# Where the projection's quanta stand in the orders of TensorE, ScalarE and VectorE

## The reference

```python
xn = rmsnorm(x, norm_mix_pre)
p = (xn @ w_in).astype(f32)                      # 256 x 2048 by 2048 x 18912
...
y_a = ...   # RWKV-7 time mixing: 32 heads of 64, a recurrence over the frames
y_b = ...   # gated DeltaNet: 16 heads of 128, chunks of 64 frames, a triangular solve in each
x = x + rmsnorm((sigmoid(gA) * y_a + sigmoid(gB) * y_b) @ w_out, norm_mix_post)
x = x + rmsnorm(SwiGLU(rmsnorm(x)))              # inner width 5632
```

## Time and profile before

| | |
|---|---|
| median of 3 runs (lowest, highest) | 2269.91 us (2266.4, 2270.58) |
| the profiled execution: time, span | 2271.85 us, 2270.1 us |
| TensorE busy | 2101.4 us, 93% of the span |
| VectorE, ScalarE, GpSimd busy | 1414.1, 1083.0, 158.8 us |
| granted clock of TensorE, mean | 0.963 of full |
| units 1 to 15 begin at | 162.77, 240.75, 320.29, ... 1182.82, 1262.33 us |
| from one unit's start to the next, units 1 to 14 | 78.0 us (nine), 79.5 us (five) |

### The profile page before, as it was taken

The page is one execution under the profiler, slowest core; times in us unless marked ns, Lnnn a source line. Parts: engine busy times, 40 slices in busy tenths (PEclk is TensorE's granted clock), DMA queues, the critical chain, the costliest instruction groups (busy, mean ns, idle before and its releaser), DMA issues. The chain is left out here.

```text
span 2270.1 us, 48877 instructions
## 1 busy us (share of the span) xinstructions
PE 2101.4 (93%) x20323; PEld 1800.4 (79%) x20323; DVE 1414.1 (62%) x2786; ACT 1083.0 (48%) x2015; POOL 158.8 (7%) x277
## 2 busy tenths in 40 slices
PE   5999999999999999999999849679999999999995
PEld 5888888888888888888888737558888888878884
DVE  5568777877877787777778644444445445444444
ACT  4545555555565555546555423344444444434443
POOL 3001011011101110110111010000000000000000
PEclk9999999999999999999999859879999999999998
DMA  6654454444454454444454017156555555545552
GB/s 197 173 142 117 117 138 126 128 123 129 116 146 117 129 133 117 124 130 128 120 143 117 6 39 259 56 187 193 193 185 185 185 185 188 181 151 188 191 190 93
DMA packets 382119, 327.20 MB, mean 144 GB/s; under 512 B 11280, under 2 KB 322032, under 8 KB 375280
## 3 DMA queue, kind: packets, MB, share of 16 engines
q1 hardware_dynamic: 367872, 318.53, 47.5%
q10 hardware_dynamic: 14064, 6.04, 1.1%
HBM read 322.44 MB, written 2.10 MB: 143 GB/s over the span
## 5 line engine op out<-in xcount | busy, mean ns | idle before, releaser
L1525 DVE TENSOR_TENSOR wlo<-wr,whi 128x1024 fp32r<-128x1024 f32 x296 | 362.6, 1226 | 435.0 <-ACT whi L1520 435.0
L232 PE MATMUL ps<-hi,xh 128*128 128x384 f32 (+1 forms) x1568 | 565.6, 361 | 31.9 <-ACT pu L258 29.2
L1520 ACT ACTIVATE whi<-wr 128x1024 fp32r<-128x1024 f32 x296 | 313.7, 1061 | 492.2 <-PE ps L1538 484.1
L234 PE MATMUL ps<-hi,xl 128*128 128x384 f32 (+1 forms) x1568 | 532.8, 340 | 0.0
L233 PE MATMUL ps<-lo,xh 128*128 128x384 f32 (+1 forms) x1568 | 531.7, 339 | 0.0
L227 DVE TENSOR_TENSOR lo<-raw,hi 128x768 fp32r<-128x768 f32 (+1 forms) x400 | 378.2, 965 | 122.1 <-ACT hi L222 121.4
L222 ACT ACTIVATE hi<-raw 128x768 fp32r<-128x768 f32 (+1 forms) x400 | 327.8, 834 | 219.4 <-PE ps L234 212.7
L232 PEld LDWEIGHTS ps<-hi,xh 128*128 128x128 f32 x1568 | 297.0, 189 | 67.9 <-ACT pu L258 36.4
L1534 PE MATMUL ps<-whi,xh 128*128 128x512 f32 x832 | 328.5, 395 | 20.4 <-DVE wlo L1525 20.4
L1536 PE MATMUL ps<-wlo,xh 128*128 128x512 f32 x832 | 326.9, 393 | 0.0
L1538 PE MATMUL ps<-whi,xl 128*128 128x512 f32 x832 | 326.7, 393 | 0.0
(11 more groups left out here) (284 smaller groups left out, 2324.5 us busy)
## 6 DMA issues: line engine op xcount, KB each, us to landing
raw<-in_w_in SPq DMA_DIRECT2D x288, 512.0 KB, 5.7
wr<-in_ffn_w_gate SPq DMA_DIRECT2D x44, 1024.0 KB, 5.1
wr<-in_ffn_w_up SPq DMA_DIRECT2D x44, 1024.0 KB, 5.1
wr<-in_ffn_w_down SPq DMA_DIRECT2D x22, 2048.0 KB, 7.5
wr<-in_w_out SPq DMA_DIRECT2D x16, 1024.0 KB, 5.1
raw<-in_w_in SPq DMA_DIRECT2D x8, 448.0 KB, 7.0
xt<-in_x SPq DMA_DIRECT2D x2, 1024.0 KB, 6.2
g2s<-in_rwkv_g ACTq DMA_DIRECT2D x16, 128.0 KB, 5.7
```

The lines of the kernel that those rows point to most:

```text
L232: nc.tensor.matmul(o, xh[:, kc, xs], high, start=kc == 0, stop=False)
L234: return nc.tensor.matmul(o, xl[:, kc, xs], high, start=False, stop=kc == KC - 1)
L1520: nc.scalar.activation(whi[s.par][:], src, ACT.Copy).then_inc(s.hi, 1)
L1525: nc.vector.tensor_tensor(wlo[s.par][:], src, whi[s.par][:].bitcast(F32), ALU.subtract).then_inc(s.lo, 1)
```

## The change

The same 24 quanta per unit and engine are given out to other places. No instruction is added, dropped or altered. On TensorE one quantum moves; on ScalarE and VectorE several do. The diff, cut to what moves:

```diff
 def mix_pe(pe, u, prev, more):
-                after_y, after_x = (1, 2, 1, 0, 1), (1, 1, 1, 1, 2)
+                after_y, after_x = (1, 2, 1, 1, 1), (1, 1, 1, 0, 0)
...                                        # behind the loop over the levels:
+                fill(2)
 def mix_act(act, u, prev, more):
-                before_y, before_x = (1, 1, 3, 0, 0), (0, 0, 2, 0, 2)
+                before_y, before_x = (0, 1, 7, 0, 0), (0, 0, 0, 0, 0)
...
-                fill(1)                   # at the unit's start
...
+                fill(1)                   # behind "uv" and "cv"
...
                 fn("tq", ...)
-                fill(2)
+                fill(3)
...
-                fill(1)                   # behind "winc"; another one behind "ege"
...
                 fn("edt", dd[:], dd[:], ACT.Exp)
-                fill(1)
+                fill(2)
...
                 chunk(3, 3)
+                fill(1)
...
                 fn("bt", ...)
-                fill(2)
...
                 fn("v", ...)
+                fill(1)
...
                     load_gate(act, u)
-                fill(1)
+                fill(2)
 def mix_dve(dve, u, prev, more):
-                after_y, after_x = (2, 2, 0, 1), (2, 0, 1, 1)
+                after_y, after_x = (2, 3, 0, 0), (1, 0, 1, 0)
...
                 ts("kx", ...)
+                fill(1)
...
                 conv(2, 1, "k", 2, T)
-                fill(1)
...
                 chunk(1, 2)
-                fill(2)
+                fill(1)
...
                 chunk(3, 2)
-                fill(1)
+                fill(2)
...
                     masked(f"tb{h}", tr[hp, 0:4, :, :], h, hp)
-                fill(1)
+                fill(2)
...
-                fill(2)
-                fill(1)
+                fill(4)                   # behind the loop over the levels
```

More of the change, by code:

```diff
@@ L1380, in mix_dve @@
                         output(i + 1)
-                fill(2)
-                fill(1)
+                fill(4)
                 after(A, "gates")
```

## The result

The changed kernel takes 2273.22 us (median of 20 runs, 2271.27 to 2277.7), the kernel before 2270.22 (20 runs, 2266.4 to 2274.05): ratio 1.0015, 95% interval 1.0009 to 1.0022. It is slower by 3.0 us, where 1.0 was forecast. In a later pair of the same two kernels the ratio was 1.0016 (1.0007 to 1.0026), so the difference is real though small.

A forecast was written before the change was run, and what follows sets the result against it. TensorE, busy 990.76 of 1020.00 us, was taken as the bound. Terms of +0.05 us per unit over 15 units, plus 0.18 in the last, gave +1.0 us: 2271 against the median of 2269.91, range 2265 to 2278.

The forecast's parts named there:

- The idle time at X3: TensorE in the solve: quantum 38 moved ahead of X3 saves 0.23 us per unit, bounds 0.18 to 0.28.
- X3 to Y4: TensorE in the solve: this stretch takes 1.00 us in the new order, with a wait of 0.18 ahead of Y4.
- sg: VectorE: one more `lo` ahead of sg makes TensorE's chunk 1 start 0.18 us later per unit, bounds 0.08 to 0.23.
- Rhg of chunk 3: VectorE: two `lo` behind chunk 2 delay this step, costing TensorE 0.01 us per unit, bounds 0 and 0.1.
- Quantum 32: Its `hi` and `lo` ahead of g delay squares and copy out: 0.09 us more per unit, bounds 0 to 0.28.
- the price of the `lo`: VectorE: a `lo` was taken to hold the engine for 0.87 us.
- Rival 1: Slower: three `lo` between y1 and x1 on VectorE make Y2 late, up to 2277.6 us; slower cases together 25 in 100.
- A margin of 0.66: Time in us that x1 on VectorE was to have left before TensorE wants it for Y2.
- The sum of a steady unit: All terms of one unit together: -0.23 + 0.18 + 0.01 + 0.09 = +0.05 us.
- Unit 0: The unit without chunks and with another slack, counted like the others, with 1 us either way.
- the first `hi`: Moved behind `cv`, it delays VectorE's first `lo` into idle time ahead of chunk 0; cost put at nothing.
- over a microsecond: Slack ahead of Y0: xi done this long before TensorE comes to it, so Y0 was not to be late.

## Why the forecast held, and where its steps did not

**The idle time at X3.** The mechanism was right, the size a little high. 0.23 was forecast, with bounds of 0.18 and 0.28. From Y3 to Y4 0.19 came, 0.03 of it because the quantum between them took 2.28 and not 2.31. TensorE's order alone, at 2.31, takes 3.89 from Y3 to Y4, 0.16 less than before, and 0.21 less in the whole unit. X3 to Y4 was put at 1.00 and takes 1.05.

**sg.** Right in mechanism and within its bounds: +0.18 forecast, +0.15 in the profile, 0.14 given back when the `lo` goes. Rhg of chunk 3: no wait, as against 0.01.

**Quantum 32.** The mechanism was right and the size off: 0.09 forecast, 0.24 measured beyond what TensorE brings along (the quantum comes at 50.52 into the unit, 50.13 before, of which 0.15 are from sg). xm starts at 1075.70, after `uv` on GpSimd (1073.73, 1.30 long) has ended, and takes 0.36, as assumed. The Trainium skill, in "SBUF — State Buffer", section "Who interferes with whom", says that a VectorE instruction with two SBUF inputs contends with a GpSimd instruction that reads SBUF. The trace agrees: 0.36 clear of `uv`, and 0.54 and 0.70 beside it. But xm lost only 0.18 in the kernel before, where it overlapped `uv` by 0.32. What failed was the price of the `lo`. I took 0.87, start to start. The one ahead of `g` holds VectorE for 0.99 (1072.65 to 1073.64), and `g` was 1.16 late beyond sg's 0.15, not 1.02. The squares and the copy were late by the same 0.14 to 0.15 more.

**Y2.** Rival 1 did not come, by little, and that is luck. A margin of 0.66 was worked out; the third `lo` cost 0.55 more than its 0.87 (4.03 in all against 2.61), and 0.14 was left. With the `lo` of quantum 32 back between y0 and Y2, it came, at 0.11.

**The sum of a steady unit.** By its terms it is -0.20 + 0.15 + 0.24 = +0.19, and the run with unit 0 restored shows it, 78.20. In the first profile of the changed kernel it is 78.05, because quanta behind small groups from quantum 32 on took 2.28 to 2.29 there (1096.98 to 1099.27), not 2.31. So +0.05 was met there by luck, by two errors that cancel: the sum was 0.14 short, and such quanta ran 0.03 shorter, some five in a unit. In the other profile of the changed kernel they vary between the two; the kernel before, profiled again, has 2.31 and 78.00 once more.

**Unit 0.** This is the step that failed: "unit 0 has no chunks and another slack, and I let it count as the others, with 1 us either way". It costs 2.2 us in waits, more than twice that 1 us, and one edit alone, the first `hi`, makes unit 0 1.5 longer (its cost I had set at nothing because the timeline has idle time ahead of chunk 0; in unit 0 it has not). A stretch at half clock comes on top in both profiles of the changed kernel, 1.3. With unit 0 in the old order no loss is left to be measured. The wait of 1.11 ahead of Y0 was in reach too: there, `g` and its chain have no cover of "over a microsecond". That the time still came within 0.2% is partly luck: unit 0 counts once, a steady unit fourteen times, and what a steady unit loses beyond the forecast, up to 2 us in all, was covered in the profiled executions by shorter quanta and by fewer stretches at half clock.

**The clock.** I took the five longer units of before as given. They come only with the wait at quantum 24, and their number goes from two to six in kernels that don't touch it. That moves the time by 3 to 4 us, as much as the whole change. So "moving quanta can win only its idle time" was too narrow: putting the copies first won 7.6 us of half clock beyond the idle time.

## What to carry to other kernels

Work the unit without a predecessor through by itself: an instruction that is free behind other work has a price where that work is missing. When a full engine waits, read the longest wait of the unit first, and ask of each member in its chain whether it must stand there; a `hi` and a chunk step put behind the copies were worth some 20 us, refitting the quanta around them nothing. And below half a per cent, count the stretches at a lower clock in both profiles before a difference is put down to the edit.

## What the hardware showed beyond that

A wait of 0.89 us on an engine that is busy for 97% of the time can be followed by 3.4 us at half clock, at a price of 1.5 us; none of the waits of 0.42 to 0.72 in units 1 to 14 was. A `lo` of 128x768 holds VectorE for 0.87 us ahead of most instructions and for 0.98 to 0.99 ahead of `g`, ahead of the copy `vn<-ps` and, in the kernel before, in one place ahead of `rhg`. All of these read what another engine made, but so does `nrm<-ps,eps` in the kernel before, which starts after 0.87 to 0.88; the cause stays open. Why the quanta behind small groups take 2.28 us in some executions and 2.31 in others stays open.
